# A mixture-of-experts block and an RWKV block on one core: two staging slots fewer, `lin` in SBUF, one `sq` for the whole kernel

## The chip, the cores and the metric

One Trainium2 chip, one core, the whole program in one launch. The metric is the device time in microseconds. Chip and core have a matrix engine (TensorE, PE in the profile, with its weight loads as PEld), VectorE (DVE), ScalarE (ACT), GpSimd (POOL), and SyncE (SP), which here only issues transfers; 16 DMA engines carry all of them.

## What is computed

512 tokens of width 1024 in float32 go through two blocks.

```
# first block
mod = silu(c) @ w_mod + b_mod              # shift, scale and gate, twice
h   = rms_norm(x) * (1 + scale1) + shift1
y   = hybrid_mixer(h)                      # dilated attention, gated linear attention
x   = x + gate1 * rms_norm(y)
h   = rms_norm(x) * (1 + scale2) + shift2
# router: top 4 of 32 experts for each token, softmax over the four
for each expert e, for its tokens:
    gu    = h @ w_gate_up[e] + b_gate_up[e]          # 1024 x 2048
    x_glu = min(gu[:, ::2], 7);  x_lin = clip(gu[:, 1::2], -7, 7)
    act   = x_glu * sigmoid(1.702 * x_glu) * (x_lin + 1)
    out   = act @ w_down[e] + b_down[e]              # 1024 x 1024
x   = x + gate2 * rms_norm(weighted sum of the four outs)
# second block
z   = rmsnorm(x) @ w_in_2                  # pooling branch, RWKV-7 time mix, gates
x   = x + concat(...) @ w_out_2
out = rmsnorm(x)
```

## The kernel before, in words

The program runs in stages, one after another with a barrier between them: `stage_front` and the mixers, the router, `stage_experts`, `stage_second`, `stage_rwkv`.

The expert stage works in *units*: 32 slots (tokens) of one expert. An expert with n tokens has n/32 units, rounded up, at least one; with these inputs there are 80 units for 32 experts, between one and seven for an expert. The weights of an expert come in 12 *chunks* of 128 x 2048 float32, 1 MB each: 8 of `w_gate_up`, 4 of `w_down`. They are transferred once for each expert, whatever its number of units, in the order of the experts.

The chunks land in `staging`, a circle of `STAGED` slots of 8 KB a partition. Chunk m goes to slot m modulo `STAGED`. The SP queue issues chunk m (L1667) when chunk m - `STAGED` has been used for the last time, that is, in the last unit of its expert (`free`, a wait for `chunk_done`, which the last matmul of a chunk in L1758 or L1781 counts up). After each issue SP waits until chunk m-4 has landed and then counts `chunk_in` up (`arrived`, L1651). So some five chunks are under way at a time. The first six chunks are loaded ahead, in the router stage, into the same place (`early`).

In each unit TensorE does eight chunks up (L1758), then the four chunks down of the unit before (L1781), then two transposes of the hidden rows (L1767) and of the coming rows (L1735), and the bias (L1745). A quarter of each chunk is read from `staging`, the other three from `ring`, four slots that VectorE (L1883) and ScalarE (L1816) fill by copying out of `staging`; a fill waits for `chunk_in`. Of the result of the up part, VectorE makes `lin` (L1892, clip of the linear half), ScalarE `glu` (L1822), VectorE multiplies the two (L1898). GpSimd gathers the rows of a unit (L1683, an indirect transfer, two units ahead) and stores its results (L1699 and L1702).

`stage_second` begins with 16 indirect transfers on GpSimd (L2345) that gather the expert rows of each token; TensorE weighs them (L2164). SP loads constants: after a wait for one of these gathers come two weight slices, then `BLOCK` (L2126) and the chunk masks `tri` (L2127), then small ones.

Constants: `square_constants` holds seven squares of 128 x 128: `IDENT`, `BLOCK`, `ONES`, `CUM`, `SUF`, `BEFORE`, `CAUSAL`. Before, `ident` is a tile of its own that stays for the whole kernel; the other six (`sq`) live until the router stage ends, and in the second block there is a new tile (`sq_back`) for `BLOCK` and the masks.

Of the kernel before, what the change touches and what calls it, by code (L numbers as in the profile page):

```python
# [21 lines left out]
P = 128  # L22
# [23 lines left out]
EARLY = 6  # L46
STAGED = 22
RING = 4
# [18 lines left out]

BLOCK, ONES, CUM, SUF, BEFORE, CAUSAL = range(6)
IDENT = 6
NSQ = 7  # L70
KEPT = 1


LEVEL0, PAIR_GT, SAME, LT, LE = 0, 5, 6, 7, 8
NTRI = 2 * (NSQ - 1 - KEPT)

# [133 lines left out]
def persistent(k):  # L210

    k.ident = k.sb("ident", [P, P])
    k.eps = k.sb("eps", [P, LINE])
    k.dest = k.sb("dest", [P, NT, TOPK], I32)
    k.gates = k.sb("gates", [P, NT, TOPK])
    k.gate_e = k.sb("gate_e", [P, NT, NE])
# [24 lines left out]
def stage_front(k, front):  # L241
# [3 lines left out]
    nc, d = k.nc, k.d  # L245
    k.sq = k.sb("sq", [P, NSQ - 1, P], at=front)
    k.x = k.sb("x", [P, NT, D], at=front)
# [19 lines left out]
    with ExitStack() as ctx:  # L267
# [123 lines left out]
        with nc.Block() as block:  # L391
# [31 lines left out]
            def _(act):  # L423
                act.dma_start(k.ident[:], d["square"][:, IDENT, :]).then_inc(sq_in, 16)
                act.dma_start(k.sq[:], d["square"][:, 0:NSQ - 1, :]).then_inc(sq_in, 16)
                act.wait_ge(mod_zero, 1)
# [129 lines left out]
            def _(pe):  # L556
# [55 lines left out]
                def turn(n):  # L612

                    t, part = n // 2, n % 2
                    for q in range(4):
                        at = part * S + q * P
                        mm = pe.transpose(k.bank(turn_bank[n])[:, q * P:(q + 1) * P], k.proj[:, t, at:at + P],
                                          k.ident[:])
                    mm.then_inc(turn_ps, 1)

                def turn_decayed(t):

                    for q in range(4):
                        at = QG + q * P
                        mm = pe.transpose(k.bank(decayed_bank[t])[:, q * P:(q + 1) * P], k.proj[:, t, at:at + P],
                                          k.ident[:])
                    mm.then_inc(qkdT_ps, 1)

                def beside(j, t):

                    if (j, t) == (5, 3):
                        for n in range(NT):
                            mm = pe.transpose(k.bank(2)[0:RANK, n * P:(n + 1) * P], k.proj[:, n, LR:LR + RANK],
                                              k.ident[:])
                        mm.then_inc(lr_ps, 1)
# [62 lines left out]
                shift_sums(0, 0)  # L698
                pe.wait_ge(sq_in, 32)
                for t in range(NT):  # L700
                    pe.wait_ge(normed_ready, t + 1)
                    for q in range(KT):
                        if t >= 2 and q % 4 == 0:
                            pe.wait_ge(xT_ready, 2 * (t - 2) + q // 4 + 1)
                        mm = pe.transpose(k.bank(4 + 2 * (t % 2) + q // 4)[:, (q % 4) * P:(q % 4 + 1) * P],
                                          normed(t)[:, q * P:(q + 1) * P], k.ident[:])
                        if q % 4 == 3:
                            mm.then_inc(x_turned, 1)
# [162 lines left out]
def mixers(k, front):  # L871
# [22 lines left out]
    with ExitStack() as ctx:  # L894
# [54 lines left out]
        with nc.Block() as block:  # L949
# [11 lines left out]
            def _(pe):  # L961
# [10 lines left out]
                def turn_probs(p):  # L972
                    i, m = pairs[p]
                    if p:
                        wait_copied(pe, p - 1)
                    for two in range(2):
                        pe.wait_ge(probs_ready, 2 * p + two + 1)
                        for j in range(i + 1):
                            mm = pe.transpose(k.bank(2 + two)[:, j * P:(j + 1) * P],
                                              probs[:, two, j * P:(j + 1) * P], k.ident[:])  # L980
                        mm.then_inc(probsT_ps, 1)

                def values(p):
# [12 lines left out]
                    if m == PER - 1:  # L996
                        g = p // PER
                        pe.wait_ge(inv_ready, g + 1)
                        pe.wait_ge(o_squared, min(g + 2, NT))
                        if g == NT - 1:  # L1000
                            pe.wait_ge(inv_copied, g)
                        for u in range(g * HA, (g + 1) * HA):
                            m0 = u // 2 % PER
                            mm = pe.matmul(k.bank(6)[halves[u % 2], m0 * P:(m0 + 1) * P],
                                           inv[:, u:u + 1].broadcast_to([P, DA]), k.ident[:],
                                           start=True, stop=True)
                        mm.then_inc(inv_ps, 1)
# [183 lines left out]
def stage_router(k, front):  # L1191
# [3 lines left out]
    with ExitStack() as ctx:  # L1195
# [58 lines left out]
        with nc.Block() as block:  # L1254
# [20 lines left out]
            def _(pe):  # L1275
                ident = k.ident[:]
                ones_sq = k.sq[:, ONES, :]
# [265 lines left out]
def stage_experts(k):  # L1543

    nc, d = k.nc, k.d
    with ExitStack() as ctx:
# [10 lines left out]
        rowsT = sb("rowsT", [P, 2, P])  # L1557
        lin = k.bank(1)[:, 0:GLU]
        glu = sb("glu", [P, GLU])
# [75 lines left out]
        with nc.Block() as block:  # L1635
# [91 lines left out]
            def _(pe):  # L1727
                units = units_on(pe)
                ident = k.ident[:]

# [145 lines left out]
            def _(dve):  # L1876
# [8 lines left out]
                def linear(i):  # L1885

                    dve.wait_ge(chunk_done, i * CHUNKS + KT)
                    if isinstance(i, int):
                        dve.wait_ge(pick_used, 1)
                    else:  # L1890
                        dve.wait_ge(hidden_ready, i)
                    dve.tensor_scalar(lin, k.bank(0)[:, GLU:PART], LIMIT + 1.0, 1.0 - LIMIT,  # L1892
                                      ALU.min, ALU.max).then_inc(lin_ready, 1)

                def finish_hidden(i):
                    dve.wait_ge(glu_ready, i + 1)
                    dve.wait_ge(lin_ready, i + 1)
                    dve.scalar_tensor_tensor(hidden[:], glu[:], GLU_MAX, lin, ALU.min, ALU.mult  # L1898
                                             ).then_inc(hidden_ready, 1)
# [96 lines left out]
def stage_second(k):  # L1996
# [27 lines left out]
    with ExitStack() as ctx:  # L2024
# [80 lines left out]
        with nc.Block() as block:  # L2105
            @block.sync
            def _(sp):
# [28 lines left out]
            def _(pe):  # L2136
# [4 lines left out]
                def by_block(i, src):  # L2141
                    pe.wait_ge(tri_in, 32)
                    pe.matmul(side_bank(i), k.sq[:, BLOCK, :], src, start=True, stop=True).then_inc(side_ps, 1)

                def turn_v(t):
                    pe.wait_ge(pool_scaled, t + 1)
                    for j in range(4):
                        mm = pe.transpose(side_bank(VTURN + t)[:, j * P:(j + 1) * P],
                                          v[:, j, t * P:(t + 1) * P], k.ident[:])
                    mm.then_inc(side_ps, 1)  # L2150
# [17 lines left out]
                def turn_h(t):  # L2168
                    pe.wait_ge(h_ready, t + 1)
                    for q in range(KT):  # L2170
                        if t and q % 4 == 0:
                            pe.wait_ge(hT_ready, 2 * t - 1 + q // 4)
                        mm = pe.transpose(k.bank(6 + q // 4)[:, (q % 4) * P:(q % 4 + 1) * P],
                                          h(t)[:, q // 4, (q % 4) * P:(q % 4 + 1) * P], k.ident[:])
                        if q % 4 == 3:
# [3 lines left out]
                for t in range(NT):  # L2179
                    mm = pe.transpose(k.bank(4)[0:3 * NE, t * P:(t + 1) * P],  # L2180
                                      gate_split[:, t].rearrange("p m e -> p (m e)"), k.ident[:])
                mm.then_inc(gateT_ps, 1)
# [52 lines left out]
            def _(act):  # L2235
# [33 lines left out]
                for m in range(2 * NT):  # L2269
                    act.activation(diag[:, m, :], k.ident[:], ACT.Copy,  # L2270
                                   scale=k.gates[:, m // 2, m % 2:m % 2 + 1]).then_inc(diag_ready, 1)
# [104 lines left out]
            def _(dve):  # L2376
# [115 lines left out]
                chain(dve.memset(keep[:, 0:S:CH], 0.0))  # L2492
                dve.wait_ge(tri_in, 32)
                for n, f in enumerate(tiles):
# [38 lines left out]
def stage_rwkv(k):  # L2533
# [9 lines left out]
    with ExitStack() as ctx:  # L2543
# [41 lines left out]
        alpha_of = lambda rows, j, c: k.alpha[rows, c, j, :]  # L2585
        tri = flat(k.sq[:, KEPT:, :]).rearrange("p (m n) -> p m n", n=CH)
        over_heads = lambda m: tri[:, m, :].unsqueeze(1).broadcast_to([P, HR, CH])
# [62 lines left out]
        with nc.Block() as block:  # L2650
# [14 lines left out]
            def _(pe):  # L2665
# [11 lines left out]
                def turn_solve(t):  # L2677

                    for m in range(4):
                        mm = pe.transpose(k.bank(2 * t)[:, m * P:(m + 1) * P],  # L2680
                                          solve[:, t, m].rearrange("p a n -> p (a n)"), k.ident[:])
                    mm.then_inc(solveT_ps, 1)

                def alpha_by_half(t):

                    for side in range(2):
                        out = k.bank(4 + side)[:, 4 * CH:8 * CH].rearrange("p (two a n) -> p a two n", two=2, a=2)
                        for a in range(2):
                            mm = pe.transpose(out[:, a], k.alpha[:, 2 * t + side, 2 * a:2 * a + 2, :].rearrange(  # L2689
                                "p j n -> p (j n)"), k.ident[:])  # L2690
                    mm.then_inc(prod_ps, 1)
# [29 lines left out]
                def turn(out, src):  # L2721
                    for j in range(4):
                        mm = pe.transpose(out[:, j * P:(j + 1) * P], src(j), k.ident[:])  # L2723
                    return mm
# [356 lines left out]
def build(nc, dram):  # L3081
    with ExitStack() as ctx:
        k = Core(nc, ctx, dram)
        persistent(k)
        with ExitStack() as routed:
# [73 lines left out]
```

## Time and profile before

| | us |
|---|---|
| median of three runs | 1864.23 |
| the three runs | 1863.7, 1864.23, 1865.13 |
| the profiled execution | 1864.23 |
| its span, first to last instruction | 1862.6 |
| TensorE busy in it | 1645.2 |
| VectorE, ScalarE, GpSimd busy | 1144.5, 852.7, 330.0 |

The span is what the profile shows; the time has 1.6 us around it. A busy share over the whole span mixes stages with different limits, so the rows further down are taken from stretches. A DMA share of 1.01 means that all 16 DMA engines have a transfer in each instant. PEclk is the clock that TensorE was granted, as a share of its full 2.4 GHz.

### The profile page before, as it was taken

The numbers are of one execution on the slowest core, as the hardware profiler recorded it, in microseconds if no ns is written. First come the engines' busy times: TensorE is split into PE (matmuls) and PEld (weight loads), VectorE is DVE, ScalarE is ACT, GpSimd is POOL, SyncE is SP. The second block draws the span as 40 slices with busy tenths as digits, with TensorE's granted clock in tenths as the row PEclk, the third lists the DMA queues.
The fourth block names the chain that finished last, engine by engine and source line by source line (L and its number), as shares of the span: only waits on it lengthen the run. The fifth ranks groups of instructions, "written<-read, shape, count | busy, mean of one in ns | idle before, by whom it ended". The sixth has DMA issues, their size and how long they took to land. (4 is left out here: it accounts for less than half of the span.)

```text
span 1862.6 us, 50543 instructions
## 1 busy us (share of the span) xinstructions
PE 1645.2 (88%) x16925; PEld 877.1 (47%) x16926; DVE 1144.5 (61%) x1698; ACT 852.7 (46%) x1131; POOL 330.0 (18%) x467
## 2 busy tenths in 40 slices
PE   6999889679899999989987899899887369998897
PEld 3999754423344344334422344344232147877753
DVE  4785343656577777657755577577554275964664
ACT  5334532155466666546634466555443144534411
POOL 0000000022222322212211222222121300630000
PEclk9999999789999999989989999999897679999999
DMA  9872574187979999994899999999998822211101
GB/s 336 262 250 86 169 188 171 47 364 292 425 306 399 423 423 423 423 426 183 335 425 425 425 387 419 423 426 384 424 425 371 297 64 69 81 54 48 60 2 46
DMA packets 136740, 520.86 MB, mean 280 GB/s; under 512 B 20163, under 2 KB 59092, under 8 KB 87381
## 3 DMA queue, kind: packets, MB, share of 16 engines
q1 hardware_dynamic: 118132, 487.87, 66.1%
q0 software_dynamic: 18240, 31.46, 4.7%
q8 instruction: 51, 0.84, 0.2%
q10 hardware_dynamic: 290, 0.48, 0.1%
q14 instruction: 27, 0.22, 0.0%
HBM read 494.73 MB, written 24.91 MB: 279 GB/s over the span
## 5 line engine op out<-in xcount | busy, mean ns | idle before, releaser
L1883 DVE COPY ring<-staging 128x1536 f32 (+1 forms) x638 | 598.9, 963 | 299.8 <-PE banks L1758 153.4
L1816 ACT ACTIVATE ring<-staging 128x1536 f32 (+1 forms) x319 | 472.6, 1486 | 478.3 <-PE banks L1758 243.4
L1758 PE MATMUL banks<-staging,rowsT 128*32 (+1 forms) x1268 | 595.9, 616 | 84.0 <-ACT ring L1816 48.9
L1758 PE MATMUL banks<-ring,rowsT 128*32 128x512 f32 x3840 | 605.2, 617 | 0.0
L1758 PEld LDWEIGHTS banks<-staging,rowsT 128*32 128x32 f32 x1268 | 129.1, 111 | 483.4 <-issue 478.2
L1781 PE MATMUL banks<-staging,hiddenT 128*32 x1280 | 303.0, 392 | 1.4 <-ACT hiddenT L1827 0.5
L1781 PE MATMUL banks<-ring,hiddenT 128*32 128x256 f32 x3840 | 304.0, 392 | 0.0
L1781 PEld LDWEIGHTS banks<-staging,hiddenT 128*32 128x32 f32 x1280 | 144.2, 113 | 160.2 <-issue 62.3
L1781 PEld LDWEIGHTS banks<-ring,hiddenT 128*32 128x32 f32 x3840 | 160.7, 113 | 0.0
L605 PE MATMUL banks<-w_in_hi,hT 128*128 128x256 f32 (+1 forms) x768 | 147.4, 291 | 1.7 <-issue 1.7
L1758 PEld LDWEIGHTS banks<-ring,rowsT 128*32 128x32 f32 x3840 | 145.6, 111 | 0.0
L1699 POOL COPY rows_leaving<-y_rows 128x256 f32<-128x256 f32 x80 | 33.3, 417 | 583.2 <-ACT y_rows L1839 579.6
L2230 PE MATMUL banks<-h3T,w_in_hi 128*128 128x512 f32 x400 | 129.2, 405 | 1.4 <-DVE h3T L2410 1.4
L605 PEld LDWEIGHTS banks<-w_in_hi,hT 128*128 128x128 f32 x768 | 122.6, 194 | 3.7 <-issue 3.6
L1683 POOL DMA_INDIRECT rows_landing<-h_rows,slot x81 | 105.5, 1302 | 68.5 <-POOL slot L1680 60.3
L605 PE MATMUL banks<-w_in_lo,hT 128*128 128x256 f32 (+1 forms) x384 | 109.7, 286 | 0.0
L2230 PEld LDWEIGHTS banks<-h3T,w_in_hi 128*128 128x128 f32 x400 | 75.8, 191 | 23.0 <-issue 4.1
L1702 POOL DMA_DIRECT2D expert_rows<-rows_leaving x80 | 69.0, 862 | 65.7 <-POOL rows_leaving L1699 57.5
L2230 PE MATMUL banks<-h3T,w_in_lo 128*128 128x512 f32 x200 | 78.7, 394 | 0.0
L1892 DVE TENSOR_SCALAR banks<-banks 128x256 f32<-128x256 f32 x80 | 34.6, 433 | 70.9 <-PE banks L1758 70.9
L2382 DVE TENSOR_TENSOR w_in_lo<-stage,w_in_hi 128x1024 fp32r<-128x1024 f32 x25 | 35.0, 1405 | 68.8 <-ACT w_in_hi L2263 68.7
L605 PEld LDWEIGHTS banks<-w_in_lo,hT 128*128 128x128 f32 x384 | 74.5, 194 | 1.9 <-issue 1.9
(437 smaller groups left out, 1959.4 us busy)
## 6 DMA issues: line engine op xcount, KB each, us to landing
staging<-in_w_gate_up SPq DMA_DIRECT2D x250, 1024.0 KB, 12.6
staging<-in_w_down SPq DMA_DIRECT2D x128, 1024.0 KB, 12.7
stage<-in_w_mod SPq DMA_DIRECT2D x21, 1024.0 KB, 6.1
stage<-in_w_in SPq DMA_DIRECT2D x25, 512.0 KB, 4.0
stage<-in_w_in SPq DMA_DIRECT2D x11, 1024.0 KB, 5.5
expert_rows<-rows_leaving POOLq DMA_DIRECT2D x80, 128.0 KB
expert_rows<-catT SPq DMA_DIRECT2D x1, 7936.0 KB
early<-in_w_gate_up SPq DMA_DIRECT2D x6, 1024.0 KB, 9.2
```

What stands on the lines that cost most here:

```text
L605: mm = pe.matmul(k.bank(4 + t)[:, 0:w], hT[:, a, q, tt], b[:, q, :], start=(q == 0 and a == 0 and b is hi), stop=(q == KT - 1 and a == 1))
L1683: pool.indirect_dma_start(out=out[:], out_offset=None, in_=by_quarter, in_offset=bass.IndirectOffsetOnAxis(ap=slot[:, at:at + 1], axis=0)) ...
L1699: pool.tensor_copy(leaving[:], y[:]).then_inc(y_free, 1)
L1702: pool.dma_start(store_of(n * SLOTS), leaving[:]).then_inc(y_out, 16)
L1758: mm = pe.matmul(k.bank(0)[c * SLOTS:(c + 1) * SLOTS, :], rowsT[:, q % 2, row], w, start=first and q == 0, stop=not first and q == KT - 1, ...
L1781: mm = pe.matmul(k.bank(4)[c * SLOTS:(c + 1) * SLOTS, 0:GLU], hT[:, b, m * SLOTS:(m + 1) * SLOTS], w, start=(m == 0 and b == 0), stop=(m = ...
L1816: act.activation(ring[:, pos % RING, :], staged(i, e, pos, PART, CHUNK - PART), ACT.Copy).then_inc(act_filled, 1)
L1883: dve.tensor_copy(ring[:, pos % RING, :], staged(i, e, pos, PART, CHUNK - PART)).then_inc(dve_filled, 1)
L1892: dve.tensor_scalar(lin, k.bank(0)[:, GLU:PART], LIMIT + 1.0, 1.0 - LIMIT, ALU.min, ALU.max).then_inc(lin_ready, 1)
L2230: mm = pe.matmul(k.bank(n % 4), w[:, n % NW, q, :], hT[:, b, q, :], start=(q == 0 and a == 0), stop=(q == KT - 1 and a == 2))
L2382: dve.tensor_tensor(w_lo[:, n % NW], stage[:, n % 3], w_hi[:, n % NW].bitcast(F32), ALU.subtract).then_inc(w_ready, 1)
```

## The change

`STAGED` goes from 22 to 20, so the circle in `stage_experts` has 20 slots (and `BLOCKS`, half of it, 10). `lin` gets a tile of its own in SBUF, 1 KB a partition; before it is half of PSUM bank 1. `sq` holds all seven squares and stays for the whole kernel: `ident` and `sq_back` are gone, every use of `k.ident` becomes `k.sq[:, IDENT, :]`, the start loads the squares in one transfer in place of two, and the second block loads only the masks, into the squares from `KEPT` = 2 on, since `BLOCK` is still there; the waits for `tri_in` go from 32 to 16, and the one in `by_block` is gone. The scratch for GpSimd's DMA descriptors has its default size in place of 4096 bytes.

```diff
-STAGED = 22
+STAGED = 20
...
-BLOCK, ONES, CUM, SUF, BEFORE, CAUSAL = range(6)
-IDENT = 6
+IDENT, BLOCK, ONES, CUM, SUF, BEFORE, CAUSAL = range(7)
 NSQ = 7
-KEPT = 1
+KEPT = 2
...
-    k.ident = k.sb("ident", [P, P])
+    k.sq = k.sb("sq", [P, NSQ, P])
...
-    k.sq = k.sb("sq", [P, NSQ - 1, P], at=front)
...
-                act.dma_start(k.ident[:], d["square"][:, IDENT, :]).then_inc(sq_in, 16)
-                act.dma_start(k.sq[:], d["square"][:, 0:NSQ - 1, :]).then_inc(sq_in, 16)
+                act.dma_start(k.sq[:], d["square"][:, 0:NSQ, :]).then_inc(sq_in, 16)
...
-                pe.wait_ge(sq_in, 32)
+                pe.wait_ge(sq_in, 16)
...
-        lin = k.bank(1)[:, 0:GLU]
+        lin = sb("lin", [P, GLU])
...
-                    dve.tensor_scalar(lin, k.bank(0)[:, GLU:PART], LIMIT + 1.0, 1.0 - LIMIT,
+                    dve.tensor_scalar(lin[:], k.bank(0)[:, GLU:PART], LIMIT + 1.0, 1.0 - LIMIT,
                                       ALU.min, ALU.max).then_inc(lin_ready, 1)
...
-                sp.dma_start(k.sq[:, BLOCK, :], d["square"][:, BLOCK, :]).then_inc(tri_in, 16)
-                sp.dma_start(flat(k.sq[:, KEPT:, :]), d["tri"].rearrange("p m n -> p (m n)")).then_inc(tri_in, 16)
+                sp.dma_start(flat(k.sq[:, KEPT:NSQ, :]), d["tri"].rearrange("p m n -> p (m n)")).then_inc(tri_in, 16)
...
-                    pe.wait_ge(tri_in, 32)
                     pe.matmul(side_bank(i), k.sq[:, BLOCK, :], src, start=True, stop=True).then_inc(side_ps, 1)
...
-        k.sq = k.sb("sq_back", [P, NSQ - 1, P])
...
-    nc = bacc.Bacc("TRN2", target_bir_lowering=False, num_devices=1, dynamic_dma_scratch_size=4096)
+    nc = bacc.Bacc("TRN2", target_bir_lowering=False, num_devices=1)
```

## Rows read from the trace of the kernel before

**Rows 1.** The page's first part: busy us, share, instructions of TensorE.

```profile
PE 1645.2 (88%) x16925; PEld 877.1 (47%) x16926; DVE 1144.5 (61%) x1698; ACT 852.7 (46%) x1131; POOL 330.0 (18%) x467
```

**Rows 2.** The expert stage in stretches: length, busy time, granted clock, DMA share, GB/s.

```profile
core 0: us, PE busy (x) PEld busy (x) DVE busy (x) ACT busy (x) POOL busy (x), PEclk, DMA share, GB/s
391.60:449.60 58.00, 56.58 (x614) 22.56 (x618) 41.84 (x56) 34.19 (x39) 15.74 (x23) 0.95 0.67 272
449.60:510.40 60.80, 50.32 (x544) 18.85 (x540) 34.17 (x45) 28.11 (x33) 12.60 (x20) 0.94 1.01 424
510.40:776.60 266.20, 265.13 (x3087) 109.18 (x3083) 195.42 (x253) 161.71 (x185) 75.60 (x115) 1.00 0.96 399
776.60:841.40 64.80, 53.10 (x544) 19.65 (x540) 34.09 (x45) 28.16 (x33) 13.39 (x20) 0.89 1.01 425
841.40:945.00 103.60, 103.60 (x1214) 42.75 (x1210) 76.44 (x99) 63.29 (x73) 29.29 (x45) 1.00 0.68 275
945.00:1063.40 118.40, 94.48 (x946) 33.32 (x942) 59.75 (x78) 49.25 (x57) 22.63 (x35) 0.88 1.01 425
1063.40:1167.00 103.60, 103.60 (x1214) 42.78 (x1210) 76.91 (x100) 63.31 (x73) 27.23 (x45) 1.00 0.98 405
1167.00:1235.80 68.80, 62.78 (x678) 23.72 (x674) 42.42 (x56) 35.18 (x41) 16.80 (x25) 0.93 1.01 425
1235.80:1293.30 57.50, 57.50 (x678) 23.71 (x674) 42.65 (x55) 35.12 (x41) 15.06 (x25) 1.00 0.95 392
1293.30:1433.00 139.70, 111.45 (x1076) 37.13 (x1072) 67.90 (x89) 56.97 (x65) 26.08 (x40) 0.85 1.01 425
```

**Rows 3.** SP's waits in 390:440, 510:590, 840:915, 1095:1125, 1255:1285: total, times, longest.

```profile
SPq L1667 <- PE banks L1758: 28.9, 6, 27.3
SPq L1667 <- PE banks L1758: 32.2, 12, 19.6
SPq L1667 <- PE banks L1758: 44.3, 7, 42.4
SPq L1667 <- PE banks L1758: 11.6, 6, 9.8
SPq L1667 <- PE banks L1758: 11.9, 4, 10.8
```

**Rows 4.** Short stretches late in those waits, columns as in rows 2.

```profile
413.20:433.00 19.80, 19.80 (x244) 8.46 (x236) 15.01 (x20) 11.13 (x15) 5.48 (x8) 1.00 0.08 21
528.40:540.00 11.60, 11.60 (x142) 4.81 (x138) 8.52 (x13) 7.05 (x9) 3.29 (x6) 1.00 0.14 28
860.00:894.00 34.00, 34.00 (x405) 14.02 (x397) 24.89 (x32) 20.59 (x24) 9.69 (x15) 1.00 0.09 24
1114.30:1116.30 2.00, 2.00 (x24) 0.58 (x20) 1.31 (x3) 0.31 (x1) 1.19 (x2) 1.00 0.50 66
1275.00:1277.20 2.20, 2.20 (x24) 0.65 (x20) 1.50 (x3) 0.46 (x2) 1.31 (x3) 1.00 0.20 22
```

**Rows 5.** SP's chunk issues in 920:1095 and in 650:776: duration ns, first and last start.

```profile
L1667 SPq DMA_DIRECT2D staging<-in_w_gate_up x47: 327/332/333, 922.7 to 1093.0; - x47
L1667 SPq DMA_DIRECT2D staging<-in_w_down x21: 202/332/333, 920.2 to 1075.0; - x21
...
DMA to landing us min/median/max: 12.0/12.6/13.8
...
L1667 SPq DMA_DIRECT2D staging<-in_w_gate_up x32: 328/332/333, 650.6 to 775.0; - x32
L1667 SPq DMA_DIRECT2D staging<-in_w_down x16: 328/332/333, 655.9 to 758.6; - x16
```

**Rows 6.** Operations that write and read `lin` (ns, first and last start), and ScalarE's wait.

```profile
L1892 DVE TENSOR_SCALAR banks<-banks x80: 426/433/433, 391.6 to 1433.0; 128x256 f32<-128x256 f32 x80
...
L1898 DVE SCALAR_TENSOR_TENSOR glu<-glu,banks x80: 412/414/421, 392.5 to 1434.2; 128x256 f32<-128x256 f32 x80
...
ACT glu L1822 <- DVE banks L1892: 12.0, 16, 1.2
```

**Rows 7.** TensorE's wait for the first gathers of the second block.

```profile
PE banks L2164 <- DMA mixer<-expert_rows,dest: 7.1, 2, 3.8
```

More of the change, by code:

```diff
@@ L65 @@
 NCOL1 = 4 * KT
-BLOCK, ONES, CUM, SUF, BEFORE, CAUSAL = range(6)
-IDENT = 6
+IDENT, BLOCK, ONES, CUM, SUF, BEFORE, CAUSAL = range(7)
 NSQ = 7
-KEPT = 1
+KEPT = 2
 LEVEL0, PAIR_GT, SAME, LT, LE = 0, 5, 6, 7, 8
-NTRI = 2 * (NSQ - 1 - KEPT)
+NTRI = 2 * (NSQ - KEPT)
 def square_constants():
@@ L617, in turn @@
                         mm = pe.transpose(k.bank(turn_bank[n])[:, q * P:(q + 1) * P], k.proj[:, t, at:at + P],
-                                          k.ident[:])
+                                          k.sq[:, IDENT, :])
                     mm.then_inc(turn_ps, 1)
@@ L625, in turn_decayed @@
                         mm = pe.transpose(k.bank(decayed_bank[t])[:, q * P:(q + 1) * P], k.proj[:, t, at:at + P],
-                                          k.ident[:])
+                                          k.sq[:, IDENT, :])
                     mm.then_inc(qkdT_ps, 1)
@@ L633, in beside @@
                             mm = pe.transpose(k.bank(2)[0:RANK, n * P:(n + 1) * P], k.proj[:, n, LR:LR + RANK],
-                                              k.ident[:])
+                                              k.sq[:, IDENT, :])
                         mm.then_inc(lr_ps, 1)
@@ L705, in _ @@
                         mm = pe.transpose(k.bank(4 + 2 * (t % 2) + q // 4)[:, (q % 4) * P:(q % 4 + 1) * P],
-                                          normed(t)[:, q * P:(q + 1) * P], k.ident[:])
+                                          normed(t)[:, q * P:(q + 1) * P], k.sq[:, IDENT, :])
                         if q % 4 == 3:
@@ L979, in turn_probs @@
                             mm = pe.transpose(k.bank(2 + two)[:, j * P:(j + 1) * P],
-                                              probs[:, two, j * P:(j + 1) * P], k.ident[:])
+                                              probs[:, two, j * P:(j + 1) * P], k.sq[:, IDENT, :])
                         mm.then_inc(probsT_ps, 1)
@@ L1004, in values @@
                             mm = pe.matmul(k.bank(6)[halves[u % 2], m0 * P:(m0 + 1) * P],
-                                           inv[:, u:u + 1].broadcast_to([P, DA]), k.ident[:],
+                                           inv[:, u:u + 1].broadcast_to([P, DA]), k.sq[:, IDENT, :],
                                            start=True, stop=True)
@@ L1275, in _ @@
             def _(pe):
-                ident = k.ident[:]
+                ident = k.sq[:, IDENT, :]
                 ones_sq = k.sq[:, ONES, :]
@@ L1728, in _ @@
                 units = units_on(pe)
-                ident = k.ident[:]
+                ident = k.sq[:, IDENT, :]
                 def turn_rows(i, src=rows):
@@ L1897, in finish_hidden @@
                     dve.wait_ge(lin_ready, i + 1)
-                    dve.scalar_tensor_tensor(hidden[:], glu[:], GLU_MAX, lin, ALU.min, ALU.mult
+                    dve.scalar_tensor_tensor(hidden[:], glu[:], GLU_MAX, lin[:], ALU.min, ALU.mult
                                              ).then_inc(hidden_ready, 1)
@@ L2148, in turn_v @@
                         mm = pe.transpose(side_bank(VTURN + t)[:, j * P:(j + 1) * P],
-                                          v[:, j, t * P:(t + 1) * P], k.ident[:])
+                                          v[:, j, t * P:(t + 1) * P], k.sq[:, IDENT, :])
                     mm.then_inc(side_ps, 1)
@@ L2173, in turn_h @@
                         mm = pe.transpose(k.bank(6 + q // 4)[:, (q % 4) * P:(q % 4 + 1) * P],
-                                          h(t)[:, q // 4, (q % 4) * P:(q % 4 + 1) * P], k.ident[:])
+                                          h(t)[:, q // 4, (q % 4) * P:(q % 4 + 1) * P], k.sq[:, IDENT, :])
                         if q % 4 == 3:
@@ L2180, in _ @@
                     mm = pe.transpose(k.bank(4)[0:3 * NE, t * P:(t + 1) * P],
-                                      gate_split[:, t].rearrange("p m e -> p (m e)"), k.ident[:])
+                                      gate_split[:, t].rearrange("p m e -> p (m e)"), k.sq[:, IDENT, :])
                 mm.then_inc(gateT_ps, 1)
@@ L2269, in _ @@
                 for m in range(2 * NT):
-                    act.activation(diag[:, m, :], k.ident[:], ACT.Copy,
+                    act.activation(diag[:, m, :], k.sq[:, IDENT, :], ACT.Copy,
                                    scale=k.gates[:, m // 2, m % 2:m % 2 + 1]).then_inc(diag_ready, 1)
@@ L2492, in _ @@
                 chain(dve.memset(keep[:, 0:S:CH], 0.0))
-                dve.wait_ge(tri_in, 32)
+                dve.wait_ge(tri_in, 16)
                 for n, f in enumerate(tiles):
@@ L2585, in stage_rwkv @@
         alpha_of = lambda rows, j, c: k.alpha[rows, c, j, :]
-        tri = flat(k.sq[:, KEPT:, :]).rearrange("p (m n) -> p m n", n=CH)
+        tri = flat(k.sq[:, KEPT:NSQ, :]).rearrange("p (m n) -> p m n", n=CH)
         over_heads = lambda m: tri[:, m, :].unsqueeze(1).broadcast_to([P, HR, CH])
@@ L2680, in turn_solve @@
                         mm = pe.transpose(k.bank(2 * t)[:, m * P:(m + 1) * P],
-                                          solve[:, t, m].rearrange("p a n -> p (a n)"), k.ident[:])
+                                          solve[:, t, m].rearrange("p a n -> p (a n)"), k.sq[:, IDENT, :])
                     mm.then_inc(solveT_ps, 1)
@@ L2689, in alpha_by_half @@
                             mm = pe.transpose(out[:, a], k.alpha[:, 2 * t + side, 2 * a:2 * a + 2, :].rearrange(
-                                "p j n -> p (j n)"), k.ident[:])
+                                "p j n -> p (j n)"), k.sq[:, IDENT, :])
                     mm.then_inc(prod_ps, 1)
@@ L2722, in turn @@
                     for j in range(4):
-                        mm = pe.transpose(out[:, j * P:(j + 1) * P], src(j), k.ident[:])
+                        mm = pe.transpose(out[:, j * P:(j + 1) * P], src(j), k.sq[:, IDENT, :])
                     return mm
```

## The prediction

> **What bounds the kernel now.** I read the page first, then the expert stage in stretches, then the waits of the SP queue, which issues the weight transfers, then the transfer rate, and last the waits around `lin` and around the start of the second block.
>
> The page says that TensorE is busy for 1645.2 us of the span [rows 1], which would suggest that TensorE is the bound everywhere. The stretches say something else. The units of the expert stage run from 391.6 to 1433.0 us [rows 6], over half of the kernel, and it alternates between two regimes [rows 2]. In 841.4:945.0 and 1063.4:1167.0 TensorE is busy for the whole stretch and the granted clock is 1.00: TensorE is the bound. In 449.6:510.4, 776.6:841.4, 945.0:1063.4, 1167.0:1235.8 and 1293.3:1433.0 the DMA share is 1.01 at 424 or 425 GB/s, and TensorE stands idle for 10.5, 11.7, 23.9, 6.0 and 28.2 us (the length less the busy time): there the 16 DMA engines are the bound. The reason lies in the work: an expert costs 12 chunks of 1 MB whether it has one unit of 32 slots or several. An expert with many units lets the transfers run ahead until all the slots are full; a run of experts with few units then eats that lead.
>
> Before each starved stretch there is one in which the transfers had to stop. The SP queue's waits show it: L1667, which issues a chunk, waits for TensorE (L1758, the matmul that frees a slot) for 27.3, 19.6, 42.4, 9.8 and 10.8 us at the longest [rows 3]. In these waits the queue runs dry: in 413.2:433.0 the DMA share is 0.08, in 528.4:540.0 it is 0.14, in 860:894 it is 0.09, and in the two short ones (1114.3:1116.3 and 1275.0:1277.2) it is 0.50 and 0.20 [rows 4]. So there are five cycles of the same shape: slots full, DMA idle, then DMA without a gap until TensorE starves. The fifth starved stretch reaches to the end of the stage, so the time at which the last chunk lands sets the time at which the second block starts.
>
> **The change part by part.**
>
> *Two staging slots fewer (22 to 20).* The chunk that stops the transfers waits for chunk m-22 now and would wait for chunk m-20. The TensorE event that ends the wait is the same one (the last unit of the expert reaches its first chunk). So when the DMA restarts, it restarts two chunks further back. Nothing can make this up before TensorE starves, because from the restart to there the DMA share is 1.01 [rows 2]. Each cycle thus costs the time of two chunks. For one chunk: 68 transfers are issued from 920.2 to 1093.0, 172.8/67 = 2.58 us, and 48 from 650.6 to 775.0, 124.4/47 = 2.65 us [rows 5]; I take 2.62. Two chunks are 5.24 us.
>
> Do the cycles add up? After the first one, TensorE itself comes 5.2 us later out of the starved stretch. The next full state is reached at the old time (two chunks earlier in the sequence, two chunks' time late), and is left when TensorE frees a slot, 5.2 us later than before. The DMA gap grows by 5.2 us again, and again the restart is two chunks behind. So they add: 5 x 5.24 = 26.2 us. Several waits in a row count once if TensorE doesn't starve between them: in 510:590 SP waits 12 times at L1667, 32.2 us together [rows 3], but in 510.4:776.6 TensorE is idle for 1.1 us in all [rows 2], so this is one cycle.
>
> Is the whole of the two chunks exposed? A transfer lands 12.6 us after its issue [rows 5], nearly five chunks' time, so a wait of SP is hidden as long as it stays clearly below that. All five waits have already emptied the queue [rows 4], so each further microsecond of wait is one of an idle DMA. That is tight for the last two: they are dry for about 2 us only. If they had been covered, only the three long ones would count, 3 x 5.24 = 15.7 us. At the other side, with two slots fewer a wait that is too short to matter today may begin to empty the queue between the second and the third cycle and make one more loss: 6 x 5.24 = 31.4 us. I take five.
>
> *`lin` in SBUF instead of PSUM.* It is written once and read once in each of 80 units: 433 and 414 ns [rows 6]. The nearest rows for a version with `lin` in SBUF are these two themselves: the first writes and reads PSUM, the second reads one operand from PSUM and one from SBUF, and they differ by 19 ns. If each moved by 20 ns, 80 x 40 ns = 3.2 us of VectorE time would come or go. Almost none of it is on the path: the down-projection matmuls cover the chain linear, gate, finish. Only ScalarE waits for `lin`, 12.0 us over 16 units [rows 6], and TensorE doesn't wait for ScalarE there. I count 0, bounds -1 and +1 us. The Trainium skill (VectorE: DVE Perf Modes, the section on why PSUM operands drop a tier) says a PSUM operand keeps an operation from the faster two-port mode; the source of the first operation stays in PSUM and the second has two tensor operands, so by it too nothing would speed up, and no run here shows it.
>
> *One `sq` of seven squares that stays.* At the start one transfer of 448 KB takes the place of 64 and 384 KB; TensorE waits for both before, for one after. The same bytes, and the first transposes come after the matmuls of L565 in any case: 0. In the second block a transfer of 64 KB and one wait disappear; it stands behind the wait for the gathers and ahead of small loads, TensorE and VectorE don't wait for it: 0, at most -0.3 us (an issue takes SP 0.33 us [rows 5]).
>
> *The default scratch for GpSimd's DMA descriptors.* The trace doesn't show a ring, only what GpSimd's transfers cost. TensorE waits 7.1 us for the first gathers of the second block [rows 7]. If a larger scratch removed all of that, it would be -7.1 us; if nothing, 0. The gathers are issued one after another with no gap that looks like a full ring, and the wait is for the landing, so I take 0. The space for the two slots of 8 KB a partition goes here, to `lin` (1 KB) and to six squares that stay (3 KB); of 16 KB that leaves 12 KB more for the scratch.
>
> **Sum.** 0 + 26.2 + 0 + 0 + 0. The profiled execution took 1864.23 us (span 1862.6 and 1.6 around it), which is also the median of the three runs: 1864.2 + 26.2 = 1890.4 us, 1.4% slower.
>
> The Trainium skill bears on this from both sides, and the sum above needs neither. Perfetto Trace Analysis, in its section Optimization Strategy, says that a repeated gap on the engine that should be saturated can mean too few buffers; the five starved stretches agree. Its front page (Trainium Kernel Development and Optimization, Best Practices) asks for double-buffering so that DMA overlaps with compute; 20 slots are far more than that, and by this rule alone the change would cost nothing: 1864 us.
>
> **The rivals.**
>
> *No change (the lead is not what counts).* If 20 slots are as good as 22, the time stays at 1864 +-2 us. For it: the DMA engines have spare time in the full periods [rows 4], and in 510.4:776.6, 266 us long, TensorE is hardly short of a chunk [rows 2]. Against it: between each idle DMA and each starved TensorE there is no idle DMA in which two chunks could be caught up. It needs my reading of "full" to be wrong, for instance that SP's waits are for something else than a slot.
>
> *Faster.* The larger scratch removes the 7.1 us wait for gathers, `lin` gives 1 us and SP 0.3 us: 1864.2 - 8.4 = 1855.8 us if the slots cost nothing. It decides only if the slots cost less than 8.4 - 3.7 = 4.7 us (3.7 us is the bound below), that is, less than one of the five cycles. Nothing in the rows speaks for such a small loss.
>
> *Only the long waits count*: 1864.2 + 15.7 = 1879.9 us. For it: the last two dry spells are some 2 us, near the end of what the queue covers. Against: dry they are.
>
> *A sixth loss, or the clock*: 1864.2 + 31.4 = 1895.6 us. The mean granted clock is 0.85 to 0.94 in starved stretches and 1.00 in the others [rows 2]; longer starvation means more time at the lower level. While the DMA is the bound this is free; it costs where a stretch with several units follows.
>
> **How the numbers follow.** Five cycles, near 26 us (22 to 30): 0.76. Only the long ones: 0.08. A sixth or the clock: 0.07. No change: 0.05. Faster: 0.04. The predicted time is 1890.4 us. The range goes from 1880 (three cycles) to 1896 (six), which leaves out about 1 in 10. Three runs of this kernel lie within 1.4 us, so 0.2%, 3.7 us, is about what can be told from no change. Faster 0.04, the same 0.05, slower 0.91.
>
> **What would show it.** In the profile after: SP's five longest waits at L1667 each about 5.2 us longer; the starved stretches later by 5, 10, 16, 21 and 26 us at their ends, TensorE's idle time in the stage up from 80.4 us (the five above) by about 26; the two stretches where TensorE alone is the bound still take 103.6 us each; the second block from its first gather to the end as long as before, to within a microsecond or two. Wrong would be: the long waits of SP unchanged, or a DMA share under 1 between a restart and the next starved stretch, or a second block that is shorter by several microseconds, which would point to the scratch.

## The result, and the profile after

The changed kernel takes 1889.07 us (median of four runs, 1887.24 to 1893.47), the kernel before 1864.68 us (four runs): a ratio of 1.0133, 95% interval 1.0113 to 1.0152, or 24.4 us slower. The prediction was 1890.4 us, 26.2 us slower. The profiled execution took 1888.09 us with a span of 1886.5 us.

The expert stage in stretches, cut at the same units as [rows 2] (the columns are those of rows 2 too):

```profile
390.80:448.80 58.00, 56.44 (x614) 22.55 (x618) 42.00 (x56) 34.19 (x39) 16.15 (x23) 0.95 0.59 234
448.80:513.90 65.10, 55.08 (x540) 18.65 (x536) 34.27 (x44) 28.05 (x33) 13.51 (x20) 0.84 1.01 425
513.90:787.20 273.30, 268.49 (x3090) 109.41 (x3086) 195.49 (x254) 161.82 (x185) 75.80 (x115) 0.99 0.94 390
787.20:850.50 63.30, 53.93 (x544) 19.32 (x540) 34.28 (x45) 28.09 (x33) 14.46 (x20) 0.87 1.01 425
850.50:954.10 103.60, 103.60 (x1214) 42.74 (x1210) 76.58 (x99) 63.30 (x73) 30.00 (x45) 1.00 0.64 259
954.10:1077.00 122.90, 97.70 (x946) 33.21 (x942) 59.56 (x78) 49.24 (x57) 23.43 (x35) 0.85 1.01 425
1077.00:1180.60 103.60, 103.60 (x1214) 42.78 (x1210) 76.61 (x100) 63.33 (x73) 30.86 (x45) 1.00 0.94 387
1180.60:1252.40 71.80, 62.29 (x678) 23.09 (x674) 42.49 (x56) 35.14 (x41) 16.82 (x25) 0.95 1.01 425
1252.40:1309.90 57.50, 57.50 (x676) 23.71 (x671) 42.59 (x55) 35.12 (x41) 16.39 (x25) 1.00 0.90 368
1309.90:1455.30 145.40, 113.74 (x1076) 38.05 (x1072) 68.21 (x89) 57.01 (x65) 25.54 (x40) 0.84 1.01 425
```

Read it against [rows 2] line by line. Where TensorE alone is the bound, nothing moved: 58.0, 103.6, 103.6 and 57.5 us in both. All of the difference lies in the stretches where TensorE starves: 60.8 became 65.1; the pair 266.2 and 64.8 (behind one restart TensorE starves twice, shortly in 625:650 before and 629:660 after, then at length) became 273.3 and 63.3; 118.4 became 122.9; 68.8 became 71.8; 139.7 became 145.4. That is 4.3 + 5.6 + 4.5 + 3.0 + 5.7 = 23.1 us, one term for each of the five cycles.

SP's waits for a slot, in the stretches 390:440, 510:600, 845:925, 1100:1150 and 1265:1315 (total, times, longest):

```profile
SPq L1664 <- PE banks L1755: 34.1, 5, 32.7
SPq L1664 <- PE banks L1755: 35.8, 11, 23.4
SPq L1664 <- PE banks L1755: 49.4, 6, 47.7
SPq L1664 <- PE banks L1755: 17.3, 6, 15.6
SPq L1664 <- PE banks L1755: 15.9, 7, 14.1
```

The longest waits of [rows 3] grew by 5.4, 3.8, 5.3, 5.8 and 3.3 us. The late parts of these waits, to be set beside [rows 4]:

```profile
407.30:432.00 24.70, 24.70 (x288) 10.02 (x284) 18.05 (x24) 14.34 (x18) 7.78 (x12) 1.00 0.08 21
527.70:543.50 15.80, 15.80 (x185) 6.51 (x178) 12.06 (x15) 9.06 (x11) 4.15 (x7) 1.00 0.10 21
863.10:903.00 39.90, 39.90 (x472) 16.73 (x468) 29.50 (x39) 23.43 (x29) 11.32 (x17) 1.00 0.07 20
1122.60:1129.60 7.00, 7.00 (x98) 3.40 (x98) 5.28 (x8) 3.84 (x7) 1.02 (x3) 1.00 0.10 23
1287.50:1293.50 6.00, 6.00 (x82) 2.85 (x78) 4.70 (x7) 2.84 (x7) 0.99 (x2) 1.00 0.10 22
```

The two dry spells that were some 2 us are 7.0 and 6.0 us now. The DMA is all but idle in all five: 20 to 23 GB/s are about what GpSimd's gathers and stores come to (32 rows of 4 KB in and 32 out for each unit, so 256 KB in 11.5 us or 23 GB/s, an estimate).

### The profile page after: what moved, and what is told of

Read it like the earlier page. It is cut to its first block and busy times, and to the rows that moved or that the text cites. A ratio compares the mean times of both kernels' runs of the same rounds, so it can differ in the third digit from the quotient of the medians.

```text
span 1886.5 us, 50543 instructions
## 1 busy us (share of the span) xinstructions
PE 1660.4 (88%) x16925; PEld 878.5 (47%) x16926; DVE 1144.8 (61%) x1698; ACT 852.8 (45%) x1131; POOL 338.3 (18%) x467
## 3 DMA queue, kind: packets, MB, share of 16 engines
q1 hardware_dynamic: 117988, 487.81, 65.1%
## 5 line engine op out<-in xcount | busy, mean ns | idle before, releaser
L1755 PE MATMUL banks<-staging,rowsT 128*32 (+1 forms) x1268 | 608.1, 625 | 93.7 <-ACT ring L1813 55.4
L1755 PE MATMUL banks<-ring,rowsT 128*32 128x512 f32 x3840 | 617.6, 626 | 0.0
L1680 POOL DMA_INDIRECT rows_landing<-h_rows,slot x81 | 109.3, 1350 | 65.9 <-POOL slot L1677 65.9
L1889 DVE TENSOR_SCALAR lin<-banks 128x256 f32<-128x256 f32 x80 | 34.0, 424 | 77.9 <-PE banks L1755 77.8
## 6 DMA issues: line engine op xcount, KB each, us to landing
staging<-in_w_down SPq DMA_DIRECT2D x128, 1024.0 KB, 12.7
```

Of the source, the lines that this page charges most:

```text
L1680: pool.indirect_dma_start(out=out[:], out_offset=None, in_=by_quarter, in_offset=bass.IndirectOffsetOnAxis(ap=slot[:, at:at + 1], axis=0)) ...
L1755: mm = pe.matmul(k.bank(0)[c * SLOTS:(c + 1) * SLOTS, :], rowsT[:, q % 2, row], w, start=first and q == 0, stop=not first and q == KT - 1, ...
L1889: dve.tensor_scalar(lin[:], k.bank(0)[:, GLU:PART], LIMIT + 1.0, 1.0 - LIMIT, ALU.min, ALU.max).then_inc(lin_ready, 1)
```

## The experiments

Each run has a median of its own and one of the kernel before on the same chip, 1863.3 to 1864.9 us. "Stage" is the time from the first to the last execution of the operation that makes `lin`, in the profiled execution; it is 1041.4 us in before and 1064.4 us after the change.

### Is it the slots? `STAGED` alone

```diff
-STAGED = 22
+STAGED = 20
```

> The kernel before with STAGED = 20 and nothing else changed. Slots theory (all of the loss is the two missing slots): 24 to 25 us slower than before, 1888 to 1890 us, the last chunk lands about 22 us later than the 1439.0 us of before, and SP's five long waits for a slot are 3 to 6 us longer. Rival (the loss is a sum of several parts of the change): at most 20 us slower, because then lin, the squares or the scratch carry the rest.

1888.6 us, 1.0131 times before (1.0109 to 1.0154), 25.3 us slower. The stage:

```profile
394.80:1461.40 1066.60, 973.26 (x10526) 373.99 (x10530) 671.56 (x870) 555.58 (x631) 263.18 (x393) 0.93 0.92 382
```

The slots alone give the whole loss of the change, 25.3 us against 24.4. The loss in microseconds is 0.3 us above what was expected. SP's five longest waits grew by 3.7 to 6.3 us, and the last chunk is issued 28.2 us later than before (1454.7 and 1426.5), where its landing was expected 22 us later; 3.2 us of that are a later start of the stage (394.8 and 391.6).

### The other parts, taken back one at a time from the changed kernel

```diff
-    nc = bacc.Bacc("TRN2", target_bir_lowering=False, num_devices=1)
+    nc = bacc.Bacc("TRN2", target_bir_lowering=False, num_devices=1, dynamic_dma_scratch_size=4096)
```

> The changed kernel with the scratch for GpSimd's descriptors back at 4096 bytes; the 12 KB stay unused. Slots theory: same as the changed kernel, 1889 us within 2 us, and the 7.1 us wait of TensorE for the first gathers is there in both. Rival (the larger scratch pays part of the loss back): 3 us or more slower than the changed kernel, with a longer wait for the gathers of the second block.

1891.13 us (1885.62 to 1895.87): 2.1 us above the changed kernel, with a spread of 10 us. TensorE's waits for the first gathers, after the change, in this run and in the run with 20 slots alone, which also has the scratch of 4096 bytes:

```profile
PE banks L2159 <- DMA mixer<-expert_rows,dest: 6.9, 2, 4.6
```

```profile
PE banks L2159 <- DMA mixer<-expert_rows,dest: 6.0, 2, 3.9
```

```profile
PE banks L2164 <- DMA mixer<-expert_rows,dest: 5.6, 2, 3.9
```

In the kernel before it was 7.1 us [rows 7]. The three kernels with the small scratch have 5.6 to 7.1 us and the one with the default size 6.9, so the larger scratch does nothing for it. An effect of 2 us on the whole time can't be excluded by runs that lie 10 us apart.

```diff
-        lin = sb("lin", [P, GLU])
+        lin = k.bank(1)[:, 0:GLU]
...
```

> The changed kernel with lin back in PSUM bank 1. Slots theory: no difference that can be measured from the changed kernel (1889 us), since only some 9 ns for each of 80 operations change (433 ns before, 424 ns after the change) and they lie beside other work. Rival (lin in SBUF pays, because ScalarE waits for it): 1 us or more slower than the changed kernel.

1889.87 us (1885.38 to 1891.23), 1.0136 times before (1.0113 to 1.0159), and a stage of 1064.2 us against 1064.4: no difference. Writing `lin` takes 425 ns in SBUF and 433 in PSUM, the operation that reads it 418 and 414 ns.

```diff
-                act.dma_start(k.sq[:], d["square"][:, 0:NSQ, :]).then_inc(sq_in, 16)
+                act.dma_start(k.sq[:, 0:1, :], d["square"][:, 0:1, :]).then_inc(sq_in, 16)
+                act.dma_start(k.sq[:, 1:NSQ, :], d["square"][:, 1:NSQ, :]).then_inc(sq_in, 16)
...
-                pe.wait_ge(sq_in, 16)
+                pe.wait_ge(sq_in, 32)
```

> The changed kernel with the squares loaded at the start in two transfers, the identity first, and TensorE waiting for both, as before the change. The changed kernel reaches the expert stage 0.8 to 0.9 us earlier than the kernel before. If that comes from the one transfer in place of two, this run starts the stage 0.8 us later than the changed kernel, at the time of before; if it comes from anything else, it starts as early as the changed kernel.

One run, 1884.81 us. The first unit starts at 391.4 us, between the 390.9 of the changed kernel and the 391.6 of before. Taken alone it doesn't decide; the other profiles do. The run with 20 slots, whose start is that of the kernel before to the letter, has its first unit at 394.8, the one with `lin` in PSUM, whose start is that of the changed kernel, at 395.3. The start of the stage scatters over several microseconds whatever the code, and 0.7 us are no effect.

### Is it the transfer time of two chunks for each cycle? Fewer slots, half chunks, another order

`STAGED` 18 and 16, nothing else:

> The kernel before with 18 slots. Slots theory: another five times two chunks, 26 us, on top of slots20 less what TensorE makes up at the exits, plus a little for a sixth place (the chunks around 126) where the queue now runs dry: 1912 to 1920 us. Rival (the loss of the change is a step, for instance because 20 slots no longer hold what one expert and most of the next need): 18 slots cost about as much as 20, or far more than twice as much.

> The kernel before with 16 slots. Slots theory: 26 us more again plus the growing sixth and seventh cycle, 1940 to 1952 us. Rival as for 18 slots: no straight line in the number of slots.

| slots | median us | beyond 22 slots | stage us |
|---|---|---|---|
| 22 (before) | 1864.68 | | 1041.4 |
| 20 | 1888.6 | 25.3 | 1066.6 |
| 18 | 1913.4 | 48.5 | 1091.6 |
| 16 | 1950.9 | 86.0 | 1125.4 |

(The difference is to the kernel before on the same chip.) The second pair of slots costs about as much as the first (23.2 and 25.3 us), the third more: 37.5 us. Both times lie where they were expected. That further waits now empty the queue is read from the traces only in part: in 690:770, where SP waited 0.3 us at the longest with 22 slots, it waits 7.5, 9.0 and 9.7 us with 20, 18 and 16. There is no jump at any of these sizes, but a single cycle doesn't lose 5.24 us each time: by the starts of the units, the 25 us of stage between 20 and 18 slots fall on the five cycles as 7.2, 6.8, 3.3, 3.6 and 4.2 us, and the 33.7 us between 18 and 16 slots as 2.7, 8.6, 7.6, 5.0 and 9.8 us.

Half chunks. From chunk 22 on these two kernels transfer only half of each chunk, so they leave out half of the weights and compute something else; the work of the engines stays:

```diff
-                    sp.dma_start(staging[:, m % STAGED * CHUNK:(m % STAGED + 1) * CHUNK],
-                                 up(e, c) if c < KT else down(e, c - KT)).then_inc(raw_in[m % STAGED], 16)
+                    size = CHUNK if m < 22 else CHUNK // 2
+                    sp.dma_start(staging[:, m % STAGED * CHUNK:m % STAGED * CHUNK + size],
+                                 (up(e, c) if c < KT else down(e, c - KT))[:, 0:size]).then_inc(raw_in[m % STAGED], 16)
```

> The kernel before (22 slots), but from chunk 22 on only the first half of each chunk (1024 of 2048 columns) is transferred; the other half of a slot holds what was there, so the result isn't the reference's. All TensorE, ring and slot work is unchanged, the DMA needs half the time for each expert. Slots theory: the starved stretches go, TensorE is the bound throughout and the kernel is shorter by about the idle time of 80 us and the slow units around it (the units beyond 11.5 us sum to some 130 us in before): 1735 to 1785 us. It is the base for the next run.

> The same with 20 slots. Slots theory (two slots cost two chunks' transfer time in each cycle of full slots and starved TensorE, and nothing else): without starved stretches the two slots cost nothing, the same time as with 22 slots within 3 us. Rival (fewer slots cost by themselves, by SP's waits, by later chunk_in counts or by address arithmetic): slower than with 22 slots by 10 us or more here too.

With 22 slots 1738.44 us, with 20 slots 1746.33 us. The stage, first with 22 slots, then with 20:

```profile
397.10:1311.00 913.90, 909.67 (x10526) 373.39 (x10530) 669.45 (x869) 555.77 (x631) 273.22 (x393) 1.00 0.66 239
```

```profile
391.90:1316.80 924.90, 912.45 (x10522) 372.40 (x10523) 669.18 (x870) 555.79 (x631) 269.59 (x393) 1.00 0.66 236
```

The first time is what was expected: with less to transfer, the stage shrinks to 913.9 us. The second missed. In the time, 7.9 us is between the two theories; in the stage it is 11.0 us, which is what the rival asked for (the stage also starts 5.2 us earlier in the second profile, which hides a part). The waits for a chunk that SP has counted as landed tell where it comes from, first with 22 slots, then with 20:

```profile
DVE ring L1884 <- SPq L1651: 25.6, 38, 2.3
ACT ring L1817 <- SPq L1651: 22.3, 22, 1.5
```

```profile
ACT ring L1817 <- SPq L1651: 42.1, 26, 6.6
DVE ring L1884 <- SPq L1651: 38.9, 46, 3.5
```

The lead still runs out in 20 slots at a few places, although each chunk takes half the time; with 22 it just lasts. So this pair did not take the starvation away, as it was meant to. Where the 11.0 us lie still says something. Of the 79 units, 66 take 11.5 us (within 0.15) in both runs, and nearly all of the difference falls at 450:475 (2.0 us), 924:949 (1.9), 1214:1240 (3.0), and in the last two units (2.3 and 1.5). Two half chunks are 2.6 us (an estimate, half of the 5.24 us of the prediction). That is close to a loss of two half chunks at each starvation and speaks against a cost for each wait or each chunk, but it was read afterwards. The next pair puts it to the test.

The experts in another order, by renumbering them in the arrays handed over:

```diff
+    order = [13, 0, 3, 20, 25, 4, 7, 8, 9, 19, 24, 28, 2, 5, 6, 10, 11, 12, 14, 15, 17, 18, 21, 22, 23, 27, 1, 16, 26, 29, 30, 31]
+    for n, axis in (("router_w", 2), ("router_b", 1), ("w_gate_up", 1), ("b_gate_up", 1), ("w_down", 1), ("b_down", 1)):
+        a[n] = np.take(a[n], order, axis=axis)
```

> The kernel before (22 slots) with the experts renumbered in the arrays handed over, so that the units of an expert fall through the stage: 7, 5, 5, 4, 4, 3 (7 times), 2 (14 times), 1 (6 times). The result is the same. All slots are full for most of the first half, then the transfers run without a gap until the end: one cycle only. The DMA idles long, so it is slower than before by some 70 to 100 us. It is the base for the next run.

> The same order with 20 slots. Slots theory (two chunks, 5.2 us, for each cycle of full slots and then starved TensorE): one cycle, so 5 us slower than with 22 slots (3 to 8). Rival (each wait for a slot costs, or fewer slots cost in proportion to the experts or the chunks): about 24 us slower as in the given order, or more, since SP waits for slots far longer here.

With 22 slots 1925.36 us (1921.27 to 1928.84), with 20 slots 1930.10 us (1928.78 to 1931.09): 4.7 us for the same two slots that cost 25.3 us in the given order, and 5 was expected. The base itself missed: it is 61.5 us slower than the kernel before, where 70 to 100 were expected. The two halves of the stage, with 22 and with 20 slots (columns as in rows 2):

```profile
390.70:955.10 564.40, 562.92 (x6510) 231.53 (x6514) 415.64 (x539) 343.61 (x391) 161.12 (x243) 0.99 0.79 318
955.10:1493.30 538.20, 422.66 (x4024) 140.72 (x4020) 255.09 (x331) 211.64 (x241) 96.94 (x150) 0.84 1.01 425
```

```profile
393.10:957.40 564.30, 562.85 (x6510) 231.64 (x6514) 415.91 (x540) 343.66 (x391) 157.82 (x243) 0.99 0.78 314
957.40:1500.70 543.30, 416.21 (x4024) 140.51 (x4020) 254.30 (x331) 211.60 (x241) 100.00 (x150) 0.87 1.01 425
```

While TensorE is the bound the halves agree to 0.1 us, though SP's longest wait there grew from 50.1 to 55.6 us. The starved half is 5.1 us longer, two chunks of 2.6 us. One cycle, one loss: this is the theory's number. There are as many experts and chunks as in the given order, and SP waits longer for slots, so a loss that goes by experts, by chunks or by SP's waits would be some 25 us here too. That is excluded.

A mixed order, with 22 slots:

```diff
+    order = [10, 24, 1, 31, 9, 14, 0, 11, 6, 20, 30, 12, 3, 29, 8, 4, 21, 13, 27, 18, 2, 5, 17, 7, 15, 25, 23, 19, 16, 28, 22, 26]
...
```

> The kernel before (22 slots) with the experts renumbered so that the units are mixed: 2 3 1 1 3 2 5 2 2 4 1 2 5 1 3 3 2 7 2 2 2 2 2 3 2 4 2 3 1 3 2 1. The result is the same. Slots theory: what counts is how long the DMA stands idle (about 74 us in before). Followed through with 11.5 us for a unit and 2.62 us for a chunk, the mixed order leaves little but the wait in the expert of seven units: 10 to 25 us faster than before. Rival (the starved stretches come from the chip's transfers, not from the order): no change.

1841.61 us (1839.04 to 1842.75), 0.9875 times before (0.9860 to 0.9890): 22 us faster than the kernel before and 47 faster than the changed one. It was expected to be 10 to 25 us faster. It is the fastest of the kernels here that compute the whole block, but its order was chosen for these inputs, whose routing it knows; it shows what the order is worth, not a kernel for any input.

### How far two profiles of one kernel differ

> The kernel before, profiled once more, to see how far two profiles of one kernel differ: the start of the first unit (391.6 us), the length of the stage, and the sum of the units beyond 11.5 us (132.9 us). The changed kernel's first unit came 0.7 us earlier and its exits from starvation were 3 us shorter in all. If these are scatter, this run differs from the first profile by 1 us or more at one of these places.

One run, 1860.93 us. The whole stage, first as profiled before, then in this run:

```profile
391.60:1433.00 1041.40, 958.55 (x10526) 373.65 (x10530) 671.58 (x870) 555.31 (x631) 254.42 (x393) 0.95 0.94 391
```

```profile
392.00:1434.00 1042.00, 959.76 (x10526) 374.21 (x10530) 671.19 (x869) 555.30 (x631) 260.20 (x393) 0.95 0.94 391
```

A unit takes 11.5 us where TensorE is the bound. What the units take beyond that sums to 133.5 us here, against 132.9 in the first profile. The first unit (392.0 against 391.6) and the sum moved by less than 1 us; what moved is the part behind the stage, from the last `lin` to the end of the span: 429.6 us in the first profile, 425.3 us here, 431.2 us after the change. So in this pair the stage repeats within 1 us, and differences of some microseconds outside it are scatter. The five kernels with 20 slots and the given order scatter more: their stages take 1063.1 (small scratch), 1064.2 (`lin` in PSUM), 1064.4 (the changed kernel), 1064.5 (two loads) and 1066.6 us (slots alone).

## Why the prediction was right

**The mechanism.** The step "when the DMA restarts, it restarts two chunks further back" held in each of the five cycles, and that the cycles add up held too: the stretches in which TensorE is the bound kept their lengths, and the starved ones grew. The issues of the chunks show it directly. Counted from the first `lin` of its run, the changed kernel issues a chunk later than the kernel before by 5.3 us behind the first restart, then by 9.1, 14.6, 19.2 and 22.2 us (medians over the chunks up to the next full state; single ones lie up to 2.3 us off). Each time this is 4.8 to 5.3 us more than the lag with which TensorE left the starved stretch before it (0, 4.2, 9.8, 14.3 and 17.3 us). The run with one cycle (4.7 us) and the one with the slots alone (25.3 us) show it apart from the rest of the change.

**The size.** The term 5 x 5.24 = 26.2 us was too large by some 3 us in the profile: 23.1 us. It isn't one bad profile: against 1041.4 us before, the five kernels with 20 slots lose 21.7 to 25.2 us in the stage, none of them 26.2. The five restarts gave 5.3 + 4.8 + 4.8 + 4.9 + 4.9 = 24.7 us, so the time of two chunks was nearly right (with one cycle it was 5.1 us). What the sum left out is that TensorE leaves a starved stretch less late than the chunks come: by 1.0 us behind the first, 0.3 behind the third and 1.9 behind the fourth (behind the second it is 0.3 us later). With 0.4 us from the beginning sixth loss and 0.8 us that the last units add, this is the 23.0 us that the stage lost. The clock has a part in it. At the end of a starved stretch TensorE works off what has landed, partly at the lower clock, and how much of the lower clock falls into the last units varies. The last units of the first three starved stretches, before and after the change:

```profile
497.20:510.40 13.20, 13.20 (x142) 5.28 (x138) 8.71 (x12) 6.33 (x8) 2.98 (x5) 0.88 1.01 427
828.20:841.40 13.20, 13.20 (x142) 5.29 (x138) 8.58 (x12) 6.31 (x8) 3.73 (x5) 0.88 1.01 426
1049.90:1063.40 13.50, 13.44 (x142) 5.55 (x146) 8.65 (x12) 6.49 (x9) 3.71 (x5) 0.87 1.01 425
```

```profile
501.80:513.90 12.10, 12.10 (x138) 4.82 (x134) 8.59 (x11) 6.27 (x8) 2.99 (x5) 0.96 1.01 427
837.00:850.50 13.50, 13.50 (x142) 5.39 (x138) 8.69 (x12) 6.32 (x8) 3.00 (x5) 0.86 1.01 427
1064.70:1077.00 12.30, 12.30 (x142) 4.94 (x138) 8.54 (x12) 6.32 (x8) 3.73 (x5) 0.95 1.01 425
```

Two of three are over a microsecond shorter with a granted clock of 0.95 or 0.96 in place of 0.87 or 0.88. In the fourth stretch it is the units before: the last one longer than 11.5 us took 12.7 us and takes 11.8, the one before it 20.4 and 18.7. That this is chance is only argued: with 20 slots alone the restarts gave 25.8 us, the exits took back 2.1, and the stage's loss, 1066.6 - 1041.4 = 25.2 us, is nearly the forecast sum. No run fixes the clock, so its share stays open.

**Only the long waits count** (15.7 us) is excluded: the cycles behind the two short dry spells lost 3.0 and 5.7 us. **A sixth loss** began to show, inside the second cycle, between its short and its long starvation, not between the second cycle and the third as forecast: SP now waits 7.3 us at a stretch, and the DMA share falls to 0.76 for 3.8 us (733.5:737.3), 0.9 us of idle DMA; the lag of the issues grows by 0.4 us there, from 9.1 to 9.5. **The clock** as a further loss did not show: the stretches that follow a starved one kept their lengths. (The prediction says that the granted clock is 1.00 in all stretches that aren't starved; in 391.6:449.6 it is 0.95 [rows 2].) **No change** and **faster** are excluded by the interval.

**The other parts at 0** held: scratch, `lin` and squares, each within the scatter of the runs, which is some 2 us. ScalarE's wait for `lin` was 12.0 us and is 17.0 us, in 16 units as before, and the stage doesn't notice.

**What was to show it** held in part. SP's five longest waits were to grow by about 5.2 us each; three did (5.4, 5.3 and 5.8), two grew by 3.8 and 3.3 only. The starved stretches were to end later by 5, 10, 16, 21 and 26 us and end later by 3.5, 9.1, 13.6, 16.6 and 22.3 us (the stage itself starts 0.7 us earlier): the order is right, the forecast steps are too large. The part behind the stage was to stay within a microsecond or two and does (429.6 and 431.2 us). One sign of being wrong, a DMA share under 1 between a restart and the next starved stretch, did show, for 3.8 us; it is the beginning sixth loss. And I expected TensorE's idle time in the stage to grow by about 26 us, as much as the time. It grew from 82.9 us (1041.4 less 958.55; 80.4 of it in the five stretches) to 92.0 us (1064.4 less 972.37), by 9 only; its busy time grew by 14 us, for the same matmuls. In a starved stretch the granted clock drops, and a slow matmul fills part of the wait. That is a wrong reading of an indicator, not of the time: the stretches' lengths carry the loss, their busy shares don't.

The rule of the Trainium skill about repeated gaps on the engine that should be saturated (Perfetto Trace Analysis, Optimization Strategy) agrees with the trace: two slots fewer made the five starved stretches longer, by 23.1 us in all. The advice of the Trainium skill to double-buffer (Trainium Kernel Development and Optimization, Best Practices) is not enough here: 16 slots, far more than two, cost 86 us.

## What to carry to other kernels

When an engine starves, look for the last time before it at which the transfers had to stop for lack of space: in this kernel each slot taken away cost about the transfer time of one chunk for each such pair of a full buffer and a starvation, not for each wait or each chunk. Count the pairs in the trace, check that the DMA share is full between the two, and multiply; the product was 26.2 us here and the stages lost 21.7 to 25.2. With 16 slots the last two slots cost 37.5 us in time, so the product is too small once further waits empty the queue. Ask also whether another order of the work would make fewer pairs, which costs no memory.

## What the runs showed of the hardware that was not expected

TensorE's busy time is no measure of work while it starves. The same matmul of the up part, in two different chunks, took 1.05 us and 0.61 us in the kernel before, at the lower and at the higher clock:

```profile
1412.96 1.05 PE L1758 MATMUL banks<-staging,rowsT 128*32 x1 [4.41 <-DVE ring L1883]
...
1431.55 0.61 PE L1758 MATMUL banks<-staging,rowsT 128*32 x1 [2.21 <-ACT ring L1816]
```

In the descending order the starved half, 538 to 543 us long, has a granted clock of 0.84 and 0.87, and the one with the higher clock is the longer one, by the 5.1 us of its two chunks: while the transfers are the bound, the lower clock costs nothing that shows.
